# The opening of a two-layer backbone step: activations taken token tile by token tile, and the first projection's chunks set among the modulation units

## The reference

```python
def adaln(cond, w, b):
    return jnp.split(jax.nn.silu(cond) @ w + b, 6, axis=-1)
...
    h = rms_norm(x, p['norm1']) * (1 + sc1) + sh1
...
    (na_q, na_k, na_v, pool_in, mla_cq, mla_ckv, mla_kpe,
     swa_q, swa_k, swa_v) = jnp.split(h @ p['w_in'], offs, axis=-1)
```

## Time and profile before

| | |
|---|---|
| Median of 3 runs | 1559.54 us (1559.28 to 1560.8) |
| The profiled execution | 1559.71 us, its span 1557.9 us |
| Busy share of the span | TensorE 98%, DVE 69%, ACT 54%, POOL 8% |
| Granted TensorE clock, mean | 0.997 of full |
| Mean DMA rate | 103 GB/s over the span |

### The profile page before, as it was taken

The page is one execution under the profiler, slowest core; times in us unless marked ns, Lnnn a source line. Parts: engine busy times, 40 slices in busy tenths (PEclk is TensorE's granted clock), DMA queues, the critical chain, the costliest instruction groups (busy, mean ns, idle before and its releaser), DMA issues.

```text
span 1557.9 us, 29490 instructions
## 1 busy us (share of the span) xinstructions
PE 1521.6 (98%) x11402; PEld 1423.8 (91%) x11402; DVE 1068.3 (69%) x1847; ACT 841.9 (54%) x1473; POOL 122.9 (8%) x105
## 2 busy tenths in 40 slices
PE   6999999999999999999999999999999999999998
PEld 4778996899999999999986799769999999999998
DVE  4753378496878787887577334775778878787763
ACT  5666348676544444454457663685664544444442
POOL 1223004200000000000002310240000000000000
PEclk9999999999999999999999999999999999999999
DMA  9822524221222221312755035242122222221311
GB/s 348 295 67 24 156 78 129 90 82 43 94 82 82 67 97 56 104 59 87 255 173 192 28 54 160 87 136 68 55 82 82 82 82 82 73 91 58 102 59 68
DMA packets 148542, 159.96 MB, mean 103 GB/s; under 512 B 16364, under 2 KB 130740, under 8 KB 148404
## 3 DMA queue, kind: packets, MB, share of 16 engines
q1 hardware_dynamic: 147424, 157.79, 32.1%
q10 hardware_dynamic: 852, 0.25, 0.1%
q0 software_dynamic: 128, 0.05, 0.0%
HBM read 153.15 MB, written 4.65 MB: 101 GB/s over the span
## 4 chain that ended last, share of the span: by engine, by line
PE 86%; ACT 5%; DVE 5%; issue 2%; DMA 1%; ACTq 0%; DVEq 0%; SPq 0%
PE ps L2073 36%; PE ps L2529 21%; PE ps L2219 12%; PE ps L2545 4%; PE ps L2189 3%; PE ps L2109 2%; PE ps L2298 2%; PE ps L2052 2%; PE ps L2276 2%; PE ps L2245 1%; DVE extrema L1710 1%; ACT w_hi L933 1%; PE ps L2265 1%; PE ps L2429 1%; ACT pt_c L933 1%
## 5 line engine op out<-in xcount | busy, mean ns | idle before, releaser
L933 ACT ACTIVATE w_hi<-w_raw 128x512 fp32r<-128x512 f32 (+2 forms) x242 | 189.1, 782 | 188.6 <-PE ps L2073 99.9
L2529 PE MATMUL ps<-x_hi,w_hi 128*128 128x322 f32 x784 | 244.3, 312 | 0.6 <-DVE us L1900 0.6
L2529 PE MATMUL ps<-x_lo,w_hi 128*128 128x322 f32 x784 | 243.7, 311 | 0.0
L2529 PE MATMUL ps<-x_hi,w_lo 128*128 128x322 f32 x784 | 243.4, 310 | 0.0
L2073 PE MATMUL ps<-z_hi,w_hi 128*128 128x384 f32 (+1 forms) x1024 | 233.9, 309 | 0.0
L2073 PE MATMUL ps<-z_hi,w_lo 128*128 128x384 f32 (+1 forms) x1024 | 233.5, 309 | 0.0
L2073 PE MATMUL ps<-z_lo,w_hi 128*128 128x384 f32 (+1 forms) x1024 | 233.1, 309 | 0.0
L1406 DVE TENSOR_TENSOR w_lo<-w_raw,w_hi 128x512 fp32r<-128x512 f32 x212 | 146.8, 692 | 36.4 <-ACT w_hi L933 27.7
L2073 PEld LDWEIGHTS ps<-z_hi,w_hi 128*128 128x128 f32 x1024 | 157.3, 188 | 0.0
L2073 PEld LDWEIGHTS ps<-z_lo,w_hi 128*128 128x128 f32 x1024 | 156.4, 188 | 0.0
L2073 PEld LDWEIGHTS ps<-z_hi,w_lo 128*128 128x128 f32 x1024 | 156.2, 188 | 0.0
(11 more groups left out here) (293 smaller groups left out, 2828.6 us busy)
## 6 DMA issues: line engine op xcount, KB each, us to landing
w_raw<-in_mlp_w SPq DMA_DIRECT2D x64, 1024.0 KB, 5.3
ada_own<-in_w_ada SPq DMA_DIRECT2D x50, 512.0 KB, 4.0
w_raw<-in_w_in SPq DMA_DIRECT2D x12, 1024.0 KB, 6.5
ada_room<-in_w_ada SPq DMA_DIRECT2D x23, 512.0 KB, 8.4
ada_mix<-in_w_ada SPq DMA_DIRECT2D x17, 512.0 KB, 6.5
w_raw<-in_w_out SPq DMA_DIRECT2D x8, 768.0 KB, 4.7
w_raw<-in_w_in SPq DMA_DIRECT2D x4, 832.0 KB, 7.9
ada_first<-in_w_ada SPq DMA_DIRECT2D x6, 512.0 KB, 9.4
```

The source lines that it names most:

```text
L933: do(nc.scalar.activation(out, in_, ACT.Copy), sem)
L2529: last = M.matmul(bank(b, XW), w[r][:, k, :], x_of(x, x_name)[:, k, :], start=k == 0 and q == 0 and not more, stop=k == 3 and q == 2, skip ...
```

## The change

The sample's activations are loaded in four loads, one a token tile, each with a semaphore. A transpose step is now one token tile with all eight channel blocks (the last tile in two halves), and squaring waits for its own tile. The vector rows of layer 1 are loaded by SP in place of ACT. TensorE takes units 0 to 3 ahead of the wait for the last copies. The first weight block is split in two halves, of which the first serves chunks 0 and 1. Chunk 0 of the projection stands behind unit 9, chunk 1 behind unit 12, chunk 2 behind unit 15, and turn 3 behind chunk 2. Layer 1 keeps its order. The diff, cut to its core:

```diff
+X_STEPS = [(t, range(KC)) for t in range(NT - 1)] + [(NT - 1, range(KC // 2)), (NT - 1, range(KC // 2, KC))]
+VEC_BEHIND = {1: 0, 3: 1}
...
+        FIRST_TICKS = [(None, ("unit", k)) for k in range(16)]
+        for q, k in ((3, 16), (2, 15), (1, 8), (0, 5)):
+            FIRST_TICKS.insert(k, (("turn", q), None))
...
+        FIRST_TURN_ENDS = (0, 6, 10, 18, 20)
...
-            sp.dma_start(x_in[:, 0, :], a["x_prompt"][0]).then_inc(x_in_dma, 16)
-            sp.dma_start(x_in[:, 1:NT, :], a["x_sample"][0].rearrange("(t p) d -> p t d", p=P)).then_inc(x_in_dma, 16)
+            sp.dma_start(x_in[:, 0, :], a["x_prompt"][0]).then_inc(x_in_dma[0], 16)
+            for t in range(1, NT):
+                sp.dma_start(x_in[:, t, :], a["x_sample"][0, P * t - P:P * t, :]).then_inc(x_in_dma[t], 16)
+            for r, src, n in vector_rows(1):
+                sp.dma_start(vec_in[r:r + n, 1, :], src).then_inc(vec_dma[1], 16)
             load_adas(0, range(8))
             load_weights(0)
             load_adas(0, range(8, AFTER_X))
...
+            def split_first_hi(half):
+
+                if half == 0:
+                    act.wait_ge(w_dma[0], dma_count(0))
+                part = slice(unit_width(0) // 2 * half, unit_width(0) // 2 * (half + 1))
+                copy(w_hi[:, 0, part], w_raw[:, 0, part], w_hi_ready if half else w0_begun_hi)
...
                 else:
+                    root_x(0)
+                    ada_ticks(0, range(4))
+                    take_rstd(0)
+                    ada_ticks(0, range(4, 10))
+                    split_first_hi(0)
                     h_halves(0, range(1))
-                    ada_ticks(0, range(10, 15))
+                    split_first_hi(1)
                     h_halves(0, range(1, 4))
-                    ada_ticks(0, range(15, 20))
+                    ada_ticks(0, range(10, 18))
                     split_hi(1)
+                    ada_ticks(0, range(18, 20))
                 h_halves(2 * l, range(4, KC))
...
+                if l == 0:
+                    for c in range(4):
+                        scaled(c)
+                    ada_ticks(0, turn_slice(1, True))
+                    split_first_lo(0)
+                    lo(0)
+                    split_first_lo(1)
+                    for c in range(1, 4):
+                        lo(c)
+                    ada_ticks(0, turn_slice(2, True))
+                    scales(nrm, 4, 4)
+                    scaled(4)
+                    scaled(5)
+                    split_lo(1)
+                    scaled(6)
+                    ada_ticks(0, turn_slice(3, True))
+                    scaled(7)
+                    for c in range(4, KC):
+                        lo(c)
+                    return
...
-                do(V.tensor_copy(xT[:, c, :], trans_view(i, NTOK)), t_dve)
+                do(V.tensor_copy(xT[:, cs[0]:cs[-1] + 1, P * t:P * t + P],
+                                 trans_view(i, P * len(cs)).rearrange("p (c n) -> p c n", n=P)), t_dve)
...
-                    ada_ticks(0, range(4))
                     spread_rstd(0)
-                    ada_ticks(0, range(4, 16))
+                    ada_ticks(0, range(4, 12))
                     project_cq(0, range(1))
-                    ada_ticks(0, range(16, 19))
+                    ada_ticks(0, range(12, 15))
                     project_cq(0, range(1, 2))
+                    ada_ticks(0, range(15, 19))
+                    project_cq(0, range(2, 3))
                     ada_ticks(0, range(19, 20))
-                    project_cq(0, range(2, KC))
+                    project_cq(0, range(3, KC))
...
-            for c in range(KC):
-                transpose_step(("x", c), [(x_in[:, t, P * c:P * c + P], P * t) for t in range(NT)])
-                if c == 1:
-                    pe.wait_ge(vec_dma, 16 * 8 * DEPTH)
-                    for l in range(DEPTH):
-                        transpose_step(("vec", l), [(vec_in[0:NVEC, l, :], 0)])
+            for n, (t, cs) in enumerate(X_STEPS):
+                pe.wait_ge(x_in_dma[t], 16)
+                transpose_step(("x", n), [(x_in[:, t, P * c:P * c + P], P * (c - cs[0])) for c in cs])
+                if n in VEC_BEHIND:
+                    pe.wait_ge(vec_dma[VEC_BEHIND[n]], 16 * 8)
+                    transpose_step(("vec", VEC_BEHIND[n]), [(vec_in[0:NVEC, VEC_BEHIND[n], :], 0)])
             pe.wait_ge(cond_ready, 1)
+            ada_ticks(0, range(4))
```

More of the change, by code:

```diff
@@ L142 @@
 XW = NTOK // 2 + 2
+X_STEPS = [(t, range(KC)) for t in range(NT - 1)] + [(NT - 1, range(KC // 2)), (NT - 1, range(KC // 2, KC))]
+VEC_BEHIND = {1: 0, 3: 1}
 def psum_steps():
     proj, trans, acc = [], [], []
-    trans += [("x", c, "dve") for c in range(2)] + [("vec", l, "act") for l in range(DEPTH)]
-    trans += [("x", c, "dve") for c in range(2, KC)]
+    for n, (t, cs) in enumerate(X_STEPS):
+        trans += [("x", n, "dve")]
+        if n in VEC_BEHIND:
+            trans += [("vec", VEC_BEHIND[n], "act")]
     for l in range(DEPTH):
@@ L672, in ada_ticks_of @@
         def ada_ticks_of(first):
+            if first == 0:
+                return FIRST_TICKS
             if first % 48 == 0:
@@ L1172, in square_tokens, with take_vectors @@
             def square_tokens(t):
+                act.wait_ge(x_in_dma[t], 16)
                 do(nc.scalar.activation(x_sq[:, :], x_in[:, t, :], ACT.Square, accum_out=tok_rstd[:, t:t + 1]), x_squared)
-            def row(ap, n):
-                return ap.rearrange("(r c) -> r c", r=n)
-            for l in range(DEPTH):
[L1180 to L1187, removed]
+            def take_vectors(l):
                 i = trans_ix.at[("vec", l)]
@@ L1190, in _ @@
                 copy(vcol[:, l, :], trans_view(i, NVEC), t_act)
+            for r, src, n in vector_rows(0):
+                act.dma_start(vec_in[r:r + n, 0, :], src).then_inc(vec_dma[0], 16)
+            square_tokens(0)
+            square_tokens(1)
+            take_vectors(0)
             do(nc.scalar.activation(cexp[:, :], vcol[:, 0, R_C:R_C + 16], ACT.Exp, scale=-1.0), cond_exp)
-            for t in range(2, NT):
-                square_tokens(t)
+            square_tokens(2)
+            square_tokens(3)
+            take_vectors(1)
+            square_tokens(4)
             load_sqrt()
@@ L1541, in h_of @@
                         do(V.tensor_tensor(hf[:, c % 4, :], xT[:, c, :], rstd[:, :], ALU.mult), hf_ready)
+                if l == 0:
[18 more added lines that the diff above has]
+                    return
+                for c in range(KC):
+                    if c == 2:
+                        ada_ticks(48 * l, turn_slice(1))
+                    if c == 4:
+                        ada_ticks(48 * l, turn_slice(2))
+                        scales(nrm, 4, 4)
+                    scaled(c)
                     if c == 5:
                         ada_ticks(48 * l, turn_slice(3))
-                        if l == 0:
-                            split_lo(1)
-                    if c >= 2 and (l or c not in (2, 4, 5)):
+                    if c >= 2:
                         lo(c - 2)
@@ L1772, in _ @@
                                cexp[:, :].rearrange("p (m k) -> p m k", m=2), ALU.mult), cond_ready)
-            for c in range(4, KC):
-                take_x(c)
-            do(V.memset(hstat[:, :], 1.0))
+            for n in range(2, len(X_STEPS)):
+                take_x(n)
             for l in range(DEPTH):
@@ L2182, in project_cq @@
                     n = 45 * l + k // half
-                    pe.wait_ge(w_lo_ready, splits(n))
+                    if n == 0 and k < half // 2:
+                        pe.wait_ge(w0_begun, 1)
+                    else:
+                        pe.wait_ge(w_lo_ready, splits(n))
                     w = [x[:, n % 2, 0:half * MLA_W].rearrange("p (k c) -> p k c", k=half) for x in (w_hi, w_lo)]
```

68 lines of the change are left out of this document (35 added, 33 removed).

## The result

The changed kernel takes 1561.69 us in the median of 18 runs (1559.95 to 1565.76), the kernel before beside it 1559.22 (18 runs, 1557.71 to 1563.62). The ratio is 1.0019, 95% interval 1.0012 to 1.0025: slower by 2.5 us, just within the 0.2% that the prediction called "within", but above its range and on the other side of its forecast. The 18 times stand in two groups, ten from 1559.95 to 1561.81 and eight from 1562.88 on, and the median lies at the edge between them, so a microsecond of it should not be pressed. The profiled execution took 1563.34 us with a span of 1561.4.

A forecast was written before the change was run, and what follows sets the result against it. TensorE was busy 98%, with loads slowest in the opening. Of some 5.5 us gained before chunk 0, 0.70 stayed after the chain to chunk 4: profiled 1559.71 becomes 1559.0, median 1558.8 us, own range 1557.5 to 1560.2.

The forecast's parts named there:

- within: Whole kernel: a change of less than 0.2% (3.1 us), which a measurement can't tell from none; chance 0.79.
- Loads: Opening: five activation loads land from 4.6 to 10.1 us without per-load latency; second weight block stays at 38.2.
- the 16 us: Opening: five 512 KB loads one after the other by the skill's 2.0 us fixed cost; quoted against the cut, not adopted.
- Turning: Opening transposes and copies: last transpose near 16, units 0 to 3 at 16.0 instead of 21.64; 5.5 us gained.
- To the first chunk: From the root's spreading (18.0) to chunk 0: 9.8 us, chunk 0 near 28, about 5 us sooner.
- What is late next: Ahead of chunk 4: serial chain from the second block's landing (38.2) to 46.08; TensorE waits 2 us, ends at 57.63.
- The clock rival: Around 23 to 28 us: waits halve chunk 0's pace, end 60.1, 1561.3; chunk 1 slow too, 1564.3; chance 0.08.
- TensorE's clock: Chunk 0: forecast kept 3.04 us despite waits for units 8 and 9; the half-pace rival had chance 0.08.
- Behind 62 us: After the opening: nothing credited, nothing charged; the same engines follow each other as before, shifted.

The follow-up runs named there:

- turn 3 early: Changed kernel with turn 3 ahead of chunk 2, its reduction ahead of the second block's low part, unit 15's row copy ahead of its high part; 1560.05 us, ratio 1.0004.
- order alone: Kernel before with only the new order of chunks, units, turns and splits, old loads and turning; 1566.72 us, ratio 1.0048.
- filling ahead of unit 8: Changed kernel plus 12 matmuls of the identity on itself on TensorE between unit 7's turn and unit 8; 1559.55 us, ratio 1.0010.
- opening only: Kernel before with the new loads, turning, squaring and early units 0 to 3, old order of chunks, turns and splits; 1558.93 us, ratio 0.9998.
- low half 4 early: Against turn 3 early with filling: chunk 4's low half straight behind the second block's low part, ahead of scaling chunks 6 and 7; 1557.47 us, ratio 0.9993.
- long fillings: Changed kernel plus 24 identity matmuls between turn 1 and unit 8, and 16 between chunks 3 and 4; 1562.40 us, ratio 1.0025.
- opening with filling: Kernel before with new loads and turning, old order, plus 15 identity matmuls ahead of unit 8; 1557.38 us, ratio 0.9989.
- short chain with filling: Against turn 3 early with filling: VectorE scales only chunk 4 ahead of the block's low part, and chunks 5 to 7 after chunk 4's low half; 1560.44 us, 1.0008.
- filling ahead of chunk 4: Changed kernel plus 8 matmuls of the identity on itself between chunk 3 and chunk 4; 1561.83 us, ratio 1.0014.
- both fillings: Changed kernel plus 12 identity matmuls ahead of unit 8 and 8 ahead of chunk 4; 1558.44 us, ratio 1.0005.
- turn 3 early with filling: Changed kernel with turn 3 and its reduction moved ahead, plus 12 identity matmuls ahead of unit 8; 1559.27 us, ratio 1.0007.
- short chain: The same kernel as short chain with filling, but without the 12 identity matmuls ahead of unit 8; 1562.27 us, ratio 1.0017.

## Why the prediction was wrong, point by point

- **Loads:** right, and better than right. The five activation loads landed from 4.4 to 9.7 us, no latency was paid per load, and the second block came at 37.8. The first block came 1.0 us later than before (14.24 + 10.3 = 24.6); ScalarE waited 2.13 us for it, but VectorE's half of chunk 0 was still done at 27.98, ahead of TensorE at 28.58. The 2.0 us per transfer that the prediction quotes stand in the Trainium skill, "DMA: Bandwidth & Descriptors", "Anatomy of one DMA", for transfers that GpSimd issues; these were issued by SP, so the 16 us were no fair test of the page.
- **Turning:** the last transpose ended at 14.5, not 16; units 0 to 3 at 14.46, the spreading at 16.56. The copies of 1024 columns took 1.23 to 1.24 us, as priced (1.25); what was priced too high were the later transposes, at 1.7 to 1.8 us for eight: tiles 0 and 1 took 3.65 together, about as priced, but tiles 2 and 3 only 1.94 together and the last tile 1.06.
- **To the first chunk:** chunk 0 began at 28.58, the prediction said near 28. But what held it at the end was not VectorE's half (27.98), it was TensorE's units 8 and 9, which had waited for their loads and ran at the lower clock. An opening that is bound by loads turns an earlier start into a longer hole: 7.2 us gained at units 0 to 3 became 4.8 us at chunk 0 (33.35 before), part of which is the new order's (with the old order it was 0.8 us), and a hole of 2.86 us.
- **What is late next:** the smaller of the two steps that failed, 0.6 us. The chain to chunk 4 was started at the second block's landing, with the low part from 39.9. VectorE first reduces turn 2 and scales chunks 4 and 5, 2.7 us (39.71 to 42.35), and turn 2 follows chunk 1 on TensorE. The low part began at 42.37, and at 40.48 even where chunk 0 was fast. The clock rival had exactly this chain (2.6 us from turn 2 to the low part); the forecast did not sum it. By its own times it would have ended near 39.3, an estimate (27.8 for chunk 0, 3.04, 1.43, 3.05, 0.95 for two units, 0.43 for the turn, 2.6), and so just fitted before 39.9; with chunk 0 at 28.61, a turn of 0.60 and 2.76 us from the turn's end to the low part it ended at 40.48. Mis-sized by 0.6 us: chunk 4 at 46.68 instead of 46.08, end at 58.21 instead of 57.63.
- **TensorE's clock:** the main step that failed. The forecast priced chunk 0 at 3.04 us, as in the kernel before, and put the lower clock behind the wait for unit 8 at nothing; chunk 0 took 4.99 us, and chunk 4 began at 48.57 where it began at 46.68 with the hole filled, 1.9 us later. The rival to which the text gave 0.08 is what happened, one slow chunk: it said an end at 60.1 and 1561.3, the median is 1561.69, and the profiled end of 61.71 less the second half-clock stretch is 60.16 (48.57 + 11.59). Forecast 1558.8, 0.6 for the chain and 1.9 for the slow chunk make 1561.3. The argument against it was that "before, TensorE also had holes". It did not compare their lengths: 0.72 us at most there in the kernel before from 24 us on, 2.86 us here. It had even named the place (units 8 and 9) and did not ask how long the wait would be: unit 7 and turn 1 end at 26.09 - 2.86 = 23.2, unit 8 lands just ahead of 26.09. The Trainium skill, "TensorE: Matmul & The Clock Gate", "HAM oscillation", says that waits for loads between bursts of matmuls bring the half clock back; the placed times with and without filling agree. With the new opening and the new order, chunk 0 took 4.43 to 5.02 us in all four profiles without a filling ahead of unit 8 and 3.02 to 3.07 in all six with one. The times agree less well: the filling took the ratio from 1.0019 to 1.0010, from 1.0017 to 1.0008 (one chip) and from 0.9998 to 0.9989, but from 1.0004 to 1.0007 with turn 3 early.
- **The second half-clock stretch** (50 to 53 us in the profile) was in no case. It cost 1.6 us there: 60 matmuls in 13.14 us against 11.53 to 11.59. It did not show in the two other profiles with a hole of some 2 us there (order alone, filling ahead of unit 8), so it explains the profiled execution; that it is missing from the median is likely, but not shown.
- **Behind 62 us:** right that nothing is gained or lost. The span less the end of the 120 matmuls, for the executions profiled, is set by something else:

| half-clock stretches behind 62 us | kernels | us from the end of the 120 matmuls to the end of the span |
|---|---|---|
| 1 | opening only; order only; turn 3 early; filling ahead of unit 8; low half 4 early | 1497.5; 1497.8; 1498.2; 1497.9; 1498.2 |
| 2 | before; after; long fillings; opening with filling; short chain with filling | 1499.6; 1499.7; 1499.2; 1499.2; 1499.8 |
| 3 | filling ahead of chunk 4; both fillings; turn 3 early with filling; short chain | 1500.5; 1500.5; 1500.5; 1500.8 |

They are counted in the stretches 340 to 380, 760 to 800 and 1110 to 1150 us, where the clock reads 0.96 and not 1.00 (one of them, with the long fillings, at 93 us). Each is worth about 1.3 us. This chance of single executions is as large as what the experiments move in the opening, which is why the placed times of the chain decide here. The times bear them out in the pair on one chip, and only in part elsewhere.

How much of the median's 2.5 us is the first half-clock stretch can be told only roughly: by the ratios, filling it away took off 0.09% or 1.4 us (2.1 by the medians, resampling gives -0.1 to 3.9), both fillings 0.14% or 2.2 us (3.3 by the medians, 0.2 to 4.9). What remains open is what makes the clock fall in one execution and not in another. All five profiles with a wait of 2.7 to 4.0 us ahead of chunk 0 or unit 8 show the lower clock there; but so do one with 1.54 us, and one with the filling, behind waits of 1.06 and 0.77; and 2.1 us ahead of chunk 4 brought it once in three times. Three profiles (long fillings, filling ahead of chunk 4, low half 4 early) have one more half-clock stretch, between 14 and 19 us, behind waits of 0.60 and 0.99 to 1.00 us that the changed kernel's profile has too, at the full clock. So a wait raises the odds here, and its length alone does not decide.

## What to carry to other kernels

When a step is made earlier on an engine whose next step waits for a load, write down the hole that this makes and its length; compare it with the holes after which the trace shows the full clock, and sum the time at the lower clock too where it is longer. Follow a chain back from every input of the late step (here the turn as well as the landing) and sum each branch. If the early start can't be used, a few matmuls of no meaning in the hole are worth a trial, sized by the measured length of one and of the hole. And try the halves of a change by themselves: here one cost 7.6 us, and the other did no harm.

## What the runs showed of the hardware that I had not expected

- The lower clock also falls on stretches in which the records of TensorE show no hole at all. Windows view of the version with turn 3 early and the filling:

```profile
340.00:380.00 40.00, 40.00 (x271) 40.00 (x271) 28.54 (x50) 23.16 (x39) 0.00 (x0) 0.96 0.17 53
760.00:800.00 40.00, 38.79 (x333) 32.52 (x332) 25.14 (x43) 15.16 (x22) 0.00 (x0) 0.96 0.42 132
1110.00:1150.00 40.00, 40.00 (x271) 40.00 (x270) 26.75 (x46) 23.20 (x39) 0.00 (x0) 0.96 0.09 28
```

  TensorE is busy for 40.00 of 40 us in the stretches from 340 and from 1110 us, and the clock is below full; the places are the same in nearly every profile, how many of them show it in an execution is not.
- A float32 matmul of 128 by 128 by 128 is two records and takes 0.22 to 0.24 us at the full clock (16 records in 1.95 us, 48 in 5.36); a transpose of the same shape is one record (8 in 1.06 us).
- At the lower clock a matmul of 128 by 416 columns follows the one before after 0.35 us, at the full clock after 0.19 us, so a chunk costs 5.0 to 5.2 us instead of 2.8 to 3.1.
